# State update of an mLSTM decode step: each sequence's half-products in one 32-row group, four sequences per round, in two visits

## What is computed

```python
ws = jnp.exp(src - m_new[:, None, :])
decay = jnp.exp(b_last + m - m_new)
C_new = decay[..., None, None] * C + jnp.einsum('bsh,bshv,bshk->bhvk', ws, vb, kb)
...
hn = h_cell * lax.rsqrt(jnp.mean(h_cell * h_cell, axis=-1, keepdims=True) + EPS) * g_head.astype(jnp.float32)
y_a = jax.nn.sigmoid(o_pre) * hn * jax.nn.silu(za)
```

## Time and profile before

| | us |
|---|---|
| median of three runs | 1482.71 (1482.71 to 1483.03) |
| the profiled execution, device time | 1483.09 |
| its span from the first to the last instruction | 1481.6 |
| PE busy | 1466.3 (99%) |
| DVE busy | 880.8 (59%) |
| ACT busy | 620.1 (42%) |
| one head (of eight) | 75.6 |

### The profile page before, as it was taken

One profiled execution on the slowest core, in us unless ns is written; L12 is line 12 of the kernel. 1 busy time (PEld: TensorE's weight loads), 2 busy tenths in 40 slices (PEclk: granted clock), 3 DMA queues, 4 the chain that ended last, 5 costly groups with the idle time before them and its releaser, 6 DMA issues. The chain is left out here.

```text
span 1481.6 us, 31209 instructions
## 1 busy us (share of the span) xinstructions
PE 1466.3 (99%) x11131; PEld 1448.1 (98%) x11131; DVE 880.8 (59%) x1451; ACT 620.1 (42%) x869; POOL 190.6 (13%) x340
## 2 busy tenths in 40 slices
PE   9999999999999999999999999999999999999996
PEld 9999999999999999999999999999999999999996
DVE  7756565564434447676767677777767544545444
ACT  6433333333333334444544444544453343333442
POOL 4000000001000000304040404040412100000000
PEclk9999999999999999999999999999999999999998
DMA  7764655557555568696969696979796665655543
GB/s 230 222 160 134 181 154 169 167 145 244 185 171 179 176 188 213 160 297 162 300 167 292 166 296 171 288 184 281 185 277 166 210 184 169 183 174 187 173 157 138
DMA packets 310678, 292.14 MB, mean 197 GB/s; under 512 B 82880, under 2 KB 297608, under 8 KB 309840
## 3 DMA queue, kind: packets, MB, share of 16 engines
q1 hardware_dynamic: 291424, 243.05, 59.1%
q0 software_dynamic: 18960, 48.48, 9.7%
q10 hardware_dynamic: 256, 0.10, 0.0%
HBM read 266.11 MB, written 25.44 MB: 197 GB/s over the span
## 5 line engine op out<-in xcount | busy, mean ns | idle before, releaser
L1064 DVE TENSOR_TENSOR wlo<-raw,whi 128x1024 fp32r<-128x1024 f32 x416 | 507.7, 1223 | 534.2 <-ACT whi L800 529.1
L440 PE MATMUL ps<-xh,whi 128*128 128x288 f32 x2560 | 762.3, 298 | 0.0
L442 PE MATMUL ps<-xh,wlo 128*128 128x288 f32 x2560 | 755.5, 295 | 0.0
L441 PE MATMUL ps<-xl,whi 128*128 128x288 f32 x2560 | 754.5, 295 | 0.0
L800 ACT ACTIVATE whi<-raw 128x1024 fp32r<-128x1024 f32 x416 | 440.4, 1059 | 748.8 <-PE ps L442 718.7
L440 PEld LDWEIGHTS ps<-xh,whi 128*128 128x128 f32 x2560 | 481.4, 188 | 6.9 <-issue 6.2
L442 PEld LDWEIGHTS ps<-xh,wlo 128*128 128x128 f32 x2560 | 480.6, 188 | 0.0
L441 PEld LDWEIGHTS ps<-xl,whi 128*128 128x128 f32 x2560 | 480.3, 188 | 0.2
L441 PE MATMUL ps<-yl,whi 128*128 128x288 f32 x512 | 151.5, 296 | 0.0
L440 PE MATMUL ps<-yh,whi 128*128 128x288 f32 x512 | 150.8, 294 | 0.0
L442 PE MATMUL ps<-yh,wlo 128*128 128x288 f32 x512 | 150.6, 294 | 0.0
(11 more groups left out here) (341 smaller groups left out, 1073.8 us busy)
## 6 DMA issues: line engine op xcount, KB each, us to landing
raw<-in_w_in_dram SPq DMA_DIRECT2D x320, 512.0 KB, 4.0
raw<-in_w_pb_dram SPq DMA_DIRECT2D x32, 512.0 KB, 3.5
Cin<-in_state_mlstm_C_dram POOLq DMA_DIRECT2D x16, 1024.0 KB, 8.7
Xb<-in_state_mlstm_C_dram SPq DMA_DIRECT2D x256, 64.0 KB, 3.8
out_dram<-Cin POOLq DMA_DIRECT2D x16, 1024.0 KB, 6.0
raw<-in_w_pa_dram SPq DMA_DIRECT2D x32, 512.0 KB, 3.5
raw<-in_w_out_dram SPq DMA_DIRECT2D x32, 512.0 KB, 3.5
bcs<-rows_d POOLq DMA_DIRECT2D x8, 304.0 KB, 3.9
```

Of the source, the lines that this page charges most:

```text
L440: nc.tensor.matmul(out, whi[:, c, kk, cols], mh_[:, k, :], start=(k == 0), stop=False)
L441: nc.tensor.matmul(out, whi[:, c, kk, cols], ml_[:, k, :], start=False, stop=False)
L442: last = nc.tensor.matmul(out, wlo[:, c, kk, cols], mh_[:, k, :], start=False, stop=(k == KT - 1))
L1064: nc.vector.tensor_tensor(wlo[:, c], raw[:, c], whi[:, c].bitcast(F32), ALU.subtract).then_inc(lo_ready, 1)
```

## The change

Three things are altered, all in the head loop and its constants.

- **Rows.** `kv4` now has a sequence's four tokens repeated four times in 16 neighbouring rows, so that a 32-row group holds two sequences with all their products of halves. The masks, signs and weights become per-row factors (`v_sign`, `v_low`, `k_low`), made once. ACT writes `vm` itself, one version for the even and one for the odd sequences, and DVE adds the low halves; `vst` and the eight maskings are gone.
- **Products.** A matmul of the state update runs over 32 rows. Four sequences, one from each row group, stand side by side, each with a bank of its own. Eight matmuls make one visit. Visit 0 (sequences 0, 2, 4, 6, in banks 6, 7, 2, 3) stands after chunk 0 of za, visit 1 (1, 3, 5, 7, in banks 2 to 5) after chunk 3, ahead of the six transposes. `Cin` is loaded and stored as even and odd sequences.
- **Order.** `C_p`'s product moves from behind chunk 3 to behind chunk 2; ACT's copy of it moves from the end of the head to ahead of its split of chunk 3. DVE has four `add_state` after the split of chunk 0 and four after the split of chunk 3. PE waits for two `add_state` ahead of the numerators, and for `h_set`, four `add_state` and the copy of `C_p` ahead of visit 1.

```diff
-NEW_BANK = (2, 3, 5)
+STATE_ORDER = (0, 2, 4, 6, 1, 3, 5, 7)
+STATE_BANK = (6, 7, 2, 3, 2, 3, 4, 5)
...
-        def new_state(h, b):
-            pe.wait_ge(vm_set, 8 * h + b + 1)
-            if b >= 3:
-                pe.wait_ge(cs_ev, 8 * h + b - 2)
+        def new_states(h, visit):
             for vh in range(2):
-                last = nc.tensor.matmul(ps[:, NEW_BANK[b % 3], DH * vh:DH * vh + DH],
-                                        vm[:, b % 4, vh::2], kst[:], start=True, stop=True)
+                for n in range(4 * visit, 4 * visit + 4):
+                    b = STATE_ORDER[n]
+                    rows = rows_of(b // 2)
+                    last = nc.tensor.matmul(ps[:, STATE_BANK[n], DH * vh:DH * vh + DH], vm[rows, b % 2, vh::2],
+                                            kst[rows, :], start=True, stop=True)
             last.then_inc(cs_mm, 1)
...
                     pe.wait_ge(slot_free[1], H_USE[1] + 2 + 2 * h)
-                    for b in range(2):
-                        new_state(h, b)
+                    new_states(h, 0)
                 if c == 1:
                     pe.wait_ge(vt_ev, h + 1)
+                    pe.wait_ge(cs_ev, 8 * h + 2)
...
                 if c == 3:
                     pe.wait_ge(h_set, h + 1)
+                    pe.wait_ge(cs_ev, 8 * h + 4)
+                    pe.wait_ge(cp_ev, h + 1)
+                    new_states(h, 1)
...
+                    for par in range(2):
+                        nc.scalar.activation(vm[:, par, :], ps[:, 5, DH:2 * DH], ACT.Identity,
+                                             scale=v_sign[:, par:par + 1])
+                    nc.scalar.activation(vtok_h[:, 2, 0:DH], ps[:, 5, DH:2 * DH], ACT.Copy).then_inc(kvs_ev, 1)
...
             for c in range(CHUNKS):
+                if c == 3:
+                    act.wait_ge(cp_mm, h + 1)
+                    nc.scalar.activation(cpo[:], ps[:, 5, :].rearrange("p (v k) -> p v k", v=2),
+                                         ACT.Copy).then_inc(cp_ev, 1)
                 split_hi(H0 + 5 + 5 * h, c)
...
                 if c == 0:
-                    add_state(h, 0)
-                    of_sequence(h, 4)
-                    add_state(h, 1)
-                    of_sequence(h, 5)
+                    for n in range(4):
+                        add_state(h, n)
...
-                if c == 2:
-                    add_state(h, 4)
-                    add_state(h, 5)
+                if c == 3:
+                    for n in range(4, NB):
+                        add_state(h, n)
...
-            for b in range(6, NB):
-                add_state(h, b)
```

More of the change, by code:

```diff
@@ L128, in build @@
     mask8 = fixed("mask8", [P, NB])
+    v_sign = fixed("v_sign", [P, 2])
+    v_low = fixed("v_low", [P, 2])
+    k_low = fixed("k_low", [P, HEADS])
     eye8 = fixed("eye8", [P, HEADS])
@@ L690, in _ @@
                                      start=False, stop=True).then_inc(num_mm, 1)
-                    for b in range(2, 4):
-                        new_state(h, b)
                 if c == 2:
-                    for b in range(4, 6):
-                        new_state(h, b)
+                    for vh in range(2):
+                        for t in range(2):
+                            last = nc.tensor.matmul(ps[:, X5, DH * vh:DH * vh + DH], vtok_h[:, t, vh:DH:2],
+                                                    ktok[:, t, :], start=(t == 0), stop=(t == 1))
+                    last.then_inc(cp_mm, 1)
                 if c == 3:
                     pe.wait_ge(h_set, h + 1)
+                    pe.wait_ge(cs_ev, 8 * h + 4)
+                    pe.wait_ge(cp_ev, h + 1)
+                    new_states(h, 1)
                     for j in range(2):
@@ L1163, in gates_c @@
             nc.vector.tensor_scalar(rows_h[0:HEADS, T + S:], gy[:, T:2 * T], DH ** -0.5, None, ALU.mult)
-            nc.vector.tensor_copy(gqs4[:].rearrange("p (n s) -> p n s", s=S), bc(gqs[:, TP:T], 1, [96, P // S, S]))
+            nc.vector.tensor_copy(gqs4[32:64].rearrange("p (n s) -> p n s", s=S),
+                                  bc(gqs[32:64, TP:T], 1, [S, P // S, S]))
+            for rows in (rows_of(0), rows_of(2)):
+                nc.vector.tensor_copy(gqs4[rows].rearrange("p (b r t) -> p b r t", r=4, t=TS),
+                                      bc(gqs[rows, TP:T].rearrange("p (b t) -> p b t", t=TS), 2, [S, NB, 4, TS]))
             nc.vector.tensor_copy(rows_h[0:HEADS, T:T + S], gy[:, 2 * T:2 * T + S])
@@ L1413, in _ @@
                     dve.wait_ge(silu_k, 3 * h + 3)
-                    nc.vector.tensor_copy(kv4[:, 0].rearrange("p j (n s) -> p j n s", s=S),
-                                          bc(qk[:, 2:4, TP:T], 2, [P, 2, P // S, S])).then_inc(kv4_set, 1)
+                    for j in range(2):
+                        last = nc.vector.tensor_copy(
+                            kv4[:, 0, j].rearrange("p (b r t) -> p b r t", r=4, t=TS),
+                            bc(qk[:, 2 + j, TP:T].rearrange("p (b t) -> p b t", t=TS), 2, [P, NB, 4, TS]))
+                    last.then_inc(kv4_set, 1)
                 split_lo(H0 + 3 + 5 * h, c)
```

80 lines of the change are left out of this document (36 added, 44 removed).

## The result

The changed kernel takes **1486.18 us**, median of 11 runs (1485.89 to 1487.43); the kernel before, in the same measurement, 1482.88 (11 runs, 1482.68 to 1483.33). The ratio is 1.0023, with a 95% interval of 1.0015 to 1.0031. The change makes the kernel 3.3 us slower, where 0.9 us was forecast. That lies within the range of 1481.8 to 1489.0, but outside the forecast's own spread (1482.5 to 1485) and just outside the band of 0.2% that I had called no change.

The account below looks back on a forecast made before the run. PE, busy 99% of the span, was taken as the bound. The four places in a head sum to -0.16 + 0.47 - 1.25 + 0.82 = -0.12 us, 0.9 us longer over eight heads: median 1483.6, range 1481.8 to 1489.0.

Parts of the forecast that it names:

- The sum of the heads: Eight heads: four changed places sum to -0.12 us a head (a loss), 0.9 us longer in all.
- A: PE after chunk 0, last transpose to next matmul: 0.59 us before, 0.75 after with a visit, -0.16 us a head.
- B: PE after chunk 1, last numerator to the chunk's second matmul: 0.82 us before, 0.35 without the four products, +0.47 us.
- C: PE after chunk 2, where `C_p` now stands: 0.74 us before, 1.99 after, -1.25 us a head.
- D: PE from chunk 3's last matmul to the next head's first: 3.01 us before, 2.19 after, +0.82 instead of +1.56.
- Price of a visit: Eight side-by-side tile matmuls on PE: 0.75 us from a transpose, 0.77 from an ordinary matmul; bounds 0.36 and 1.40.
- Rival 1: A visit's eight tile loads run one after another, visit 1.40 us: 6.2 us longer, 1488.9; chance 0.18.
- rival 3: No passage for row tiles: visit 0.36 us, sum +0.05 us a head, 1482.3; chance 0.10.
- The weaker form of rival 1: A visit's loads at 0.12 us in a row but no passage: visit some 1.1 us, 1486.4; chance 0.05.
- The uncovered wait: After chunk 3, PE's next-head load waits for ACT's split, `silu` and slot signal: 2.08 us at the earliest.
- Rival 2: The slot's wait after chunk 3 does not bind: +0.62 us a head, 5.0 us shorter, 1477.7; chance 0.05.
- The edits at nothing in the head: Other new waits and moved DVE, ACT, POOL steps cost nothing; the numerators' wait is covered by 0.2 us only.

## Why the prediction was right or wrong

**The sum of the heads** was right in each of its steps. A was forecast at 0.75 us and measured at 0.75, B at 0.35 and 0.35, C at 1.99 and 1.99, D at 2.19 and 2.19. In all, 0.12 us a head were forecast and 0.14 measured.

**Price of a visit.** 0.75 us, taken from a helper with tiles of 32 columns, held for tiles of 32 rows. The view of the line of the eight products in after, loads and matmuls of all visits (min, median, max in ns):

```profile
L620 PEld LDWEIGHTS ps<-kst,vm x128: 187/191/195, 611.4 to 1156.0; 32*128 32x128 f32 x128
L620 PE MATMUL ps<-kst,vm x128: 272/333/392, 611.4 to 1156.2; 32*128 32x256 f32 x128
```

A load record of 32 rows is as long (191 ns) as one of 128 rows, but the loads of four row groups run side by side: the first four start within 0.01 us. PE's timeline of after, cut at 611.45, has only the first four matmuls of the visit; cut later it has all eight, in 0.52 us, so the second four start some 0.23 after the first. The prediction had named two groups 0.12 apart as its sign. The records of the first four, which waited for their loads, begin some 0.11 too early, as above (0.40 instead of 0.29); less that it is the 0.12:

```profile
611.40 0.40 PE L620 MATMUL ps<-kst,vm 32*128 32x256 f32 x4
```

Rival 1 (loads one after another) is thereby out, and so is rival 3: the passage is paid, 0.22 us on the way in (625.49 - 625.27) instead of 0.13. The weaker form of rival 1 had 1486.4, nearest of all to the measured time. That is chance: its visit was 1.1 us, and the measured one is 0.75.

**The uncovered wait.** ACT's split and `silu` let PE's load start 2.08 us after chunk 3, to a hundredth what was read from the earlier trace rows, since moving `C_p` leaves ACT's two steps where they were. Rival 2 was forecast at 1477.7 us; with ACT really ahead the kernel takes 1478.04 (its operands at the old place modulo 256). That rival's sum was right, its condition was not met.

**The edits at nothing in the head.** The cover of 0.2 us at the numerators held: the waits view of PE has no row for them. No row shows PE waiting for weights either.

**The step that failed** is this one: "The constants before the heads are a handful of small DVE steps while PE runs a whole pair." It prices the making of the three constants, and that is indeed nothing. It does not price their place. By lying ahead of `yh`, `yl` and `mh` they lengthen every pair that reads these by 0.05 to 0.10 us: 0.8 us before the heads and 1.0 behind them. The same 96 bytes without any constants cost the kernel before 2.0 us. The chance of 0.02 for "something that I don't see" was too small for that: the whole difference from the forecast, 1486.18 less 1482.88 less 0.9, is 2.4 us, of which the place is 1.8 to 2.0, the heads' 0.02 a head 0.2, and the rest is within the spread of the medians.

**The range** held by luck. Its upper end was there for rival 1, which the traces refute, and not for a cost outside the heads; the time lies 1.2 us above the forecast's own spread. The bound of no change was 0.2%, and the interval of the result, 0.23% [0.15, 0.31], takes it in.

## What to carry to other kernels

Where an engine is busy 99% of the time, read for every piece of work that you move which wait it covers; here 1.7 us of `C_p` covered a hand-over of two ACT steps, and the change paid only once the second step (`silu`, which frees the slot) went first. Count a new constant twice, for its making and for what it pushes: compare pairs that the change does not touch in both traces, and if they differ, shift the buffers behind it with an unused one, here to 256 bytes from the old place. A step that is taken forward on an engine delays another there, and what that one starts may be a transfer: the same move was worth 6.4 us in one kernel and cost 2.6 in the other.

## What the runs showed of the hardware

- **The place of the moving operand counts.** With the same matmuls, a shift of the operand by 64 bytes of a partition lengthens a pair of 96 matmuls ahead of the heads from 12.70 to 12.75 us, by 96 bytes to 12.80, and by 256 bytes not at all; by 128 it is 12.70 in one pair and 12.74 in seven. 64 and 96 bytes are 0.5 and 1 ns a matmul of 288 columns. Behind the heads the pairs on `yh` take 12.75 us with or without the 64 bytes, and 12.80 with the 96. What in the chip makes it so, no run here tells.
- **Passage.** A visit of eight tile matmuls of 256 columns, over four row groups, takes 0.75 us, of which seven of the eight products are 0.13 (D of 1.38 and 1.25 us). The Trainium skill (TensorEngine Tiling (Array Packing), Key Properties) has the drain at a change of mode; the rows agree for row tiles as well, with 0.22 us instead of 0.13 on the way in.
- **Order in a visit.** Two matmuls in a row on one row group don't hold up the other groups by more than 0.02 us a visit.
